# Moving five small on-chip tables from above the arena to below it in an eight-stage transformer kernel

## The reference

```
for l in range(2):                                   # first block
    p = rms_norm(x, norm_g[l]) @ w_in[l]             # 1024 -> 8776 columns
    y_a = short_conv_mixer(...) @ w_out_conv[l]
    y_b = sparse_attention_mixer(...) @ w_out_attn[l]   # top 128 keys of an index score
    y_c = pool_mixer(...) @ w_out_pool[l]
    x = x + (g0*y_a + g1*y_b + g2*y_c) @ w_o[l]
for i in range(2):                                   # second block
    u = rmsnorm(h, ln_mix[i]) @ w_in_2[i]
    mixed = g0*attention(u) + g1*hyena(u) + g2*gla(u)   # each through its own 512 -> 1024 product
    h = h + mixed @ w_out_2[i]
    h = h + memory_cross_attention(rmsnorm(h), rmsnorm(mem), ...)
    h = h + square(relu(rmsnorm(h) @ mlp_w1[i])) @ mlp_w2[i]
```

## Time and profile before

| | |
|---|---|
| median of three runs | 3804.81 us |
| the profiled execution: its own time | 3802.50 us |
| the profiled execution: span from first to last instruction | 3800.7 us |
| PE busy | 3571.3 us, 94% of the span |
| DVE, POOL, ACT busy | 1796.0, 1653.9, 1488.3 us |
| granted clock of the matrix engine, mean | 0.962 of full |
| transfers | 346.96 MB, queue 1 at 27.5% of the 16 transfer engines |
| chain that ended last | PE 78%, DVE 12%, ACT 3%, POOL 2%, DMA 1% |

### The profile page before, as it was taken

How to read it: one execution, slowest core, us unless ns; L and a number is a source line. 1 busy time by engine, 2 the same in 40 slices (tenths; PEclk the granted TensorE clock), 3 DMA queues, 4 the chain that set the end, 5 groups by cost and what they waited for, 6 DMA issues and landing times.

```text
span 3800.7 us, 41092 instructions
## 1 busy us (share of the span) xinstructions
PE 3571.3 (94%) x15836; PEld 2806.2 (74%) x15836; DVE 1796.0 (47%) x2571; ACT 1488.3 (39%) x2169; POOL 1653.9 (44%) x846
## 2 busy tenths in 40 slices
PE   8999999999998899899998999988998999989999
PEld 5777787777686676577786888866765777768887
DVE  5476444476547664444543321275644444433120
ACT  3344733334633234543544322232255445343221
POOL 4443344453344462243541555554521436325564
PEclk9999999999998999999999999989998999999999
DMA  4322234222233112121341332321221223314222
GB/s 148 102 78 80 73 106 145 94 81 84 70 105 120 58 64 75 45 68 58 120 154 56 133 107 95 116 86 53 67 67 48 69 70 129 132 58 150 97 96 94
DMA packets 121932, 346.96 MB, mean 91 GB/s; under 512 B 15998, under 2 KB 16318, under 8 KB 121736
## 3 DMA queue, kind: packets, MB, share of 16 engines
q1 hardware_dynamic: 121736, 344.33, 27.5%
HBM read 315.95 MB, written 18.87 MB: 88 GB/s over the span
## 4 chain that ended last, share of the span: by engine, by line
PE 78%; DVE 12%; ACT 3%; issue 3%; POOL 2%; DMA 1%; SPq 1%; DVEq 0%; ACTq 0%; POOLq 0%
PE B L734 23%; PE B L735 23%; PE B L736 23%; PE B L778 1%; PE B L883 1%; PE B L861 1%; PE B L1024 1%; PE B L1042 1%; POOL WSP L1376 1%; DVE XP L2020 1%; PE B L987 1%; DVE RXA L1676 1%; DVE FM L1499 1%; DVE B L1470 1%; DVE RXA L1487 1%
## 5 line engine op out<-in xcount | busy, mean ns | idle before, releaser
L1376 POOL TENSOR_TENSOR WSP<-WRAW,WSP 128x1024 fp32r<-128x1024 f32 (+1 forms) x600 | 1351.9, 2257 | 1812.8 <-ACT WSP L1057 1812.6
L734 PE MATMUL B<-H,WSP 128*128 128x512 f32 x2496 | 1016.4, 407 | 42.9 <-POOL WSP L1376 15.7
L735 PE MATMUL B<-H,WSP 128*128 128x512 f32 x2496 | 989.6, 396 | 0.0
L736 PE MATMUL B<-H,WSP 128*128 128x512 f32 x2496 | 988.3, 396 | 0.0
L1057 ACT ACTIVATE WSP<-WRAW 128x1024 fp32r<-128x1024 f32 (+1 forms) x600 | 582.9, 976 | 713.3 <-PE B L736 587.3
L734 PEld LDWEIGHTS B<-H,WSP 128*128 128x128 f32 x2496 | 480.8, 193 | 190.4 <-issue 48.8
L735 PEld LDWEIGHTS B<-H,WSP 128*128 128x128 f32 x2496 | 480.3, 192 | 102.7 <-issue 6.0
L736 PEld LDWEIGHTS B<-H,WSP 128*128 128x128 f32 x2496 | 479.1, 192 | 104.2
L1470 DVE TENSOR_TENSOR B<-B,RN 128x512 f32<-128x512 f32 x170 | 118.3, 697 | 439.5 <-PE B L736 439.4
L734 PE MATMUL B<-YM,WSP 128*128 128x512 f32 x512 | 199.4, 389 | 0.0
L736 PE MATMUL B<-YM,WSP 128*128 128x512 f32 x512 | 199.2, 389 | 0.0
(11 more groups left out here) (397 smaller groups left out, 5877.4 us busy)
## 6 DMA issues: line engine op xcount, KB each, us to landing
WRAW<-in_wb SPq DMA_DIRECT2D x318, 512.0 KB, 3.7
WRAW<-in_wa SPq DMA_DIRECT2D x154, 512.0 KB, 3.7
WRAW<-in_wa SPq DMA_DIRECT2D x48, 256.0 KB, 2.6
WRAW<-in_wb SPq DMA_DIRECT2D x48, 256.0 KB, 2.6
WRAW<-in_wd SPq DMA_DIRECT2D x16, 512.0 KB, 3.5
QA<-RXA SPq DMA_DIRECT2D x64, 64.0 KB, 2.0
PA<-xs SPq DMA_DIRECT2D x16, 256.0 KB, 2.7
xs<-PA SPq DMA_DIRECT2D x16, 256.0 KB, 4.4
```

The source lines that it names most:

```text
L734: e.matmul(o, L[0], R[0], start=first, stop=False)
L735: e.matmul(o, L[0], R[1], start=False, stop=False)
L736: return e.matmul(o, L[1], R[0], start=False, stop=last)
L1376: e.tensor_tensor(WSP[:, i % NSP, 1, 0:m], WRAW[:, i % NRAW, 0:m], WSP[:, i % NSP, 0, 0:m].bitcast(fp32), ALU.subtract).then_inc(*lo_done. ...
```

## The change

The five small tiles are made ahead of `RN` instead of behind the arena, the reserving tile `ARENA` goes, `PAR` grows from 220 to 224 columns and `EPSC` from 2 to 32 columns.

```
-ARENA = 65
-PB_COLS = 220
+PB_COLS = 224
...
         WSP = fixed("WSP", [128, NSP, 2, 1024], fp32r)
+        CST = fixed("CST", [128, 6, 128])
+        PAR = fixed("PAR", [128, PB_COLS])
+        EPSC = fixed("EPSC", [128, 32])
+        SM = fixed("SM", [128, 16, 16])
+        IW = fixed("IW", [128, 32])
         RN = fixed("RN", [128, 512])
         ACC = fixed("ACC", [128, 512])
...
-        fixed("ARENA", [128, ARENA, 512])
-        CST = fixed("CST", [128, 6, 128])
-        PAR = fixed("PAR", [128, PB_COLS])
-        EPSC = fixed("EPSC", [128, 2])
-        SM = fixed("SM", [128, 16, 16])
-        IW = fixed("IW", [128, 32])
```

## The result

The changed kernel is slower: median 3826.44 us of six runs (3818.40 to 3827.99) against 3803.55 us of the kernel before in the same comparison (six runs). The ratio is 1.0061 with a 95% interval of 1.0043 to 1.0080, so about 23 us. The forecast was 3804.3 us within 3797.5 to 3812: wrong.

What follows compares the result with a forecast made beforehand. The prediction took PE's pace through its products as the bound. All terms were 0 except -0.5 us for transfers, taking the profiled 3802.5 to 3802.0 us; 2.3 us up to the median gave 3804.3 us, range 3797.5 to 3812.

Steps and rivals of the forecast that it cites:

- What bounds the kernel: Whole kernel: PE, busy 3571.3 of 3800.7 us and 78% of the chain, sets the time by its pace through products.
- EPSC, PAR, SM: EPSC fill, PAR load: longer but covered by the wait for first weights, cost 0; SM operations: 0, within 0.6 us.
- Transfers: Transfers with an arena tile on the chain: -0.5 us from the new alignment, range -1.1 to +1.1 us.
- The eight waits on the chain: Eight arena-tile transfers on the chain, 23.2 us in sum, 9.6 us of it above the smallest transfer's time.
- DVE and POOL: Vector-engine delays beside POOL operations: cost stays as it is, term 0, if operations meet in time, not by address.
- The six pieces in cross attention: Chain pieces of line 2020 delayed beside POOL, forecast to stay near 4.78 us; near 1.4 us means the faster rival.
- the faster rival: DVE and POOL delays depend on address and could go: 20.3 us less in cross attention, 3784.5 us; chance 6 in 100.
- Products that read the arena: Lines 734 to 736, 4800 products of 389 ns: change 0, bounded by 1 ns each, 4.8 us either way.
- The slower rival: Arena products lose WSP's remainder and writers meet PE at other moments: 4 ns each, 19.2 us, 3824.0 us; 6 in 100.

Runs made afterwards that it cites:

- the padded kernel after: The changed kernel with 384 unused bytes ahead of RN, so the arena is 5632 bytes above its old place; median 3803.31 us, ratio 1.0001 to the kernel before.
- everything moved: The changed kernel with the five small tiles ahead of H too, so H, WRAW, WSP, RN, ACC and arena move up 5248 bytes; median 3800.97 us, ratio 0.9998.
- `H` alone out of step: The kernel before with 128 unused bytes between WRAW and WSP; WSP, RN, ACC and arena move, H and WRAW stay; median 3837.79 us, ratio 1.0101.

## Why the prediction was wrong

- *What bounds the kernel*: right. PE's pace sets the time; the loss is in PE's products and nearly all of it reaches the end (25.2 us of busy time, 24.3 of span).
- *EPSC, PAR, SM*: right, each at its forecast size; the padded kernel after bounds them together with all else at 1.0001 (0.9990 to 1.0012). The count behind the bound of `SM` was low: the trace of before has some 1200 instructions that read or write it, not 600, so the bound should have been 1.2 us.
- *Transfers*: the size of -0.5 us can't be seen in the median times; single waits moved by -1.3 and +0.4 us. The eight waits on the chain sum to 23.1 us before and 22.2 after. In the other traces the same sum is 22.0 to 22.9 us where the arena stays 128 past a boundary of 256 bytes (moved by 4096, 256, 512 or 5632) and 21.7 to 22.0 where it lies on one (everything moved, moved by 128, `H` alone out of step): means of 22.6 and 22.0, one execution each. That has the sign and about the size of the forecast, but is no larger than the spread of 1.1 us at one remainder, so it isn't shown. By the estimate from the Trainium skill's rule on 256-byte boundaries ("DMA: Bandwidth & Descriptors", "How a descriptor splits into AXI transactions") it would have been -1.1; these sums neither carry it nor exclude it.
- *DVE and POOL*: right. The six pieces in cross attention are still there at 4.77 to 4.82 us, while `XP` and the weights no longer have the same remainder, so the faster rival is refuted.
- *Products that read the arena*: this step failed. "Value taken: 0, since 389/389/389 is nearest", with 1 ns as the bound both ways. The rows are flat because in the kernel before both operands of each of these products had the same remainder by 256, whole tiles and 512-byte pieces alike. A flat row says how a quantity varies over what was varied, and the difference wasn't. I wrote that the rows could not show another remainder and then still took their resolution as the bound of it. It measured about 5.8 ns on `HU` and 6.4 on `YM`. Over 4992 products (my count of 4800 left out the 192 in which `MN` gives the weights) these intervals make an estimated 28 us; PE's busy time rose by 25.2 and the median by 22.9.
- *The slower rival* named this mechanism, these tiles and the lost common remainder with `WSP`, at 3824.0 us with 4 ns a product; measured were 3826.4. Its 4 ns was a guess and came out too low by about 2; it had 6 chances in 100, argued down by the same flat rows. Its second half, that the writers of the arena meet PE at other moments, has no support: the minimum rose too, and with everything moved together the writers' addresses in the arena are those of the kernel after.

What the mechanism is inside the chip isn't shown. The runs show that it depends on the pair, the remainder by 256 and the direction; that the two reads disturb each other is only the nearest reading. The Trainium skill, page "SBUF — State Buffer", section "A bandwidth-pool intuition that's wrong (but worth ruling out)", gives the matrix engine a second, independent read port for weight loads. It names no condition on the two addresses. The runs here show one, worth 2.2 to 6.6 ns on `YM` in an interval of 226.7; whether it lies in these ports isn't shown.

## What to carry to other kernels

Where a stream of 128x128 by 512 products on fp32r tiles bounds a kernel (no other type was in such a stream here), check that weights and streaming rows start at the same remainder by 256 bytes, and keep small tables out of the gap between them or pad them to a multiple of 256. When a table changes size or place, everything allocated behind it moves, so compare addresses before and after. And before a flat row serves as a bound, ask whether the thing that changes was ever different in it.

## What the runs showed of the hardware that I had not expected

- A 128x128 by 512 product on fp32r tiles in a steady stream takes 226.7 ns from start to start when both operands have the same remainder by 256 bytes, and about 232 to 233 on average when the streaming rows are 32, 128 or 192 bytes beyond the weights. With 64 bytes beyond it is 228.9 on `YM`. No other difference below 256 was run on `YM`.
- Neither the distance (4096 bytes) nor multiples of 256 (256, 512, 5632) matter.
- Products of 256 columns on the arena tile `MN` did not slow down: the median interval is 120 ns before and after. Their durations, before and after:

```profile
L736 PE MATMUL B<-MN,WSP x128: 279/283/416, 1844.1 to 3193.5; 128*128 128x256 f32 x128
```

```profile
L733 PE MATMUL B<-MN,WSP x128: 274/281/415, 1851.4 to 3211.3; 128*128 128x256 f32 x128
```
